# Where the activation tiles of a two-block fp32 transformer kernel start within 64 bytes of SBUF address

## The chip, the cores and the metric

The kernel runs on one core of a Trainium2 chip. The metric is the device time of one launch in microseconds (us); durations of single instructions are in nanoseconds (ns). Three runs of the kernel before gave 2814.7, 2814.81 and 2817.35 us; their median is 2814.81 us.

## The reference, cut to what matters

Two transformer blocks follow each other on 256 tokens of width 2048, all in float32. The first has a stick-breaking attention, a gated spatial branch and a squared-ReLU feed-forward part; the second has a modulation by projected vectors, a neighbourhood attention with a context of 256 more tokens, Fourier and Hyena mixers, and a gated feed-forward part with a short convolution:

```python
x = x + merged @ w_out
h2 = rms_norm(x, g_ff)
x = x + jnp.square(jax.nn.relu(h2 @ w_ff1)) @ w_ff2        # 2048 -> 8192 -> 2048
...
x = x + g1 * (y @ w_out)
x = x + g2 * conv_gated_mlp(modulate(rmsnorm(x, norm2_g), sh2, sc2), w_up, conv_w, conv_b, w_down)
return rmsnorm(x, final_norm_g)                            # inner width 5632
```

Nearly all the arithmetic is in the products of 256 rows of activations with large weight matrices.

## The kernel before

**Tiling.** Activations are held transposed, as tiles of 128 partitions by (chunk, 256 tokens); a chunk is one kilobyte in a partition. A weight matrix is streamed through in loads of 1 MB, [128, 4 chunks, 512 columns], each of which is one *product* (`product`, from line 1607 on). SyncE starts the load into one of four `RAW` buffers (`load`).

**Split numbers.** Each float32 operand is split into a high and a low part of type fp32r. For weights, ScalarE copies RAW to `WH` (`high_half`, line 477) and VectorE subtracts to get `WL` (line 882); both are double buffered. For activations the high parts are `XH`, `HH`, `MH`, `CH`, the low parts `XL`, `HL`, `ML`, `CL`. A product is high·high + high·low + low·high, three matmuls for each tile.

**Two forms of a product.** In `ws` (lines 1589 to 1591) a 128x128 piece of the weights is the stationary operand and 256 columns of activations move past it; a product has 4 chunks x 4 column pieces x 3 = 48 such matmuls, each with its own weight load. In `tok` (lines 1600 to 1602) a 128x128 piece of the activations is stationary and 512 columns of weights move; a product has 4 x 2 x 3 = 24 of them. In the profile's rows the moving operand's name stands first: `PS<-XH,WH` is `ws`, `PS<-WH,XH` is `tok`.

**Which tile serves where.** XH and XL hold the input of most products: projections, gates, first feed-forward matrices, the second block's w_out. HH and HL hold the hidden activations of the two feed-forward parts (`down`). MH and ML serve the first block's w_out alone, CH and CL the context's projections; in these last, one product with CH/CL and one with XH/XL take turns on the same weight tiles.

**Addresses.** Every tile lies at a place written out by hand, `at(name, shape, offset)`, 16512 bytes (258 x 64) above the start of a partition. The offsets of RAW, WH, WL, XH, XL, HH and HL are whole kilobytes. MH, ML, CH and CL lie whole kilobytes above `AR`, and `AR` is 128·1024 + 2176 + 5664, which leaves 32 when divided by 64. Rows of all these tiles and the slices of WH and WL that a matmul reads begin at multiples of 512 bytes from the tile's start.

**Order of work.** Each engine runs its own written-out program; semaphores join them. TensorE waits for `lo_done` (the weights' low half) before each half product, ScalarE waits for `pe_half` before it overwrites a WH half, VectorE waits for ScalarE. The two feed-forward parts are hardware loops over pairs of steps. Between stages a norm has to be finished (`norm_window`) before products go on.

Of the kernel before, what the change touches and what calls it, by code (L numbers as in the profile page):

```python
# [8 lines left out]
P = 128  # L9
T = 256  # L10
TT = T // P
D = 2048
KC = D // P
NB = 512
FT = NB // P
# [6 lines left out]
FNG = 4  # L22
HW = 512
# [127 lines left out]
def build_program(nc, d, out):  # L151
    f32, f32r = mybir.dt.float32, mybir.dt.float32r
# [5 lines left out]
    with ExitStack() as ctx:  # L158
        def at(name, shape, offset, dt=f32):
            return nc.alloc_sbuf_tensor_at(name, shape, dt, offset=base + offset)  # L160
# [4 lines left out]
        K = 1024  # L165
# [2 lines left out]
        WH = at("WH", [P, 2, FT, NB], 32 * K, f32r)  # L168
        WL = at("WL", [P, 2, FT, NB], 48 * K, f32r)
        X = at("X", [P, KC, T], 64 * K)  # L170
        XH = at("XH", [P, KC, T], 80 * K, f32r)
        XL = at("XL", [P, KC, T], 96 * K, f32r)
        HH = at("HH", [P, 2, FT, T], 112 * K, f32r)
        HL = at("HL", [P, 2, FT, T], 120 * K, f32r)
        NT = at("NT", [P, KC, T], 112 * K)
        CON = 128 * K
        cols = at("cols", [P, NCOLS], CON)
        small = CON + 2176
        mats = at("mats", [P, 4, P], small)
# [27 lines left out]
        lnb = at("lnb", [P, 1024], AR + 44 * K)  # L207
        bsp = at("bsp", [P, 8, P], AR + 48 * K)
        wsp = at("wsp", [P, 8, P], AR + 52 * K)
        t1 = 112 * K  # L210
        sgt = at("sgt", [P, 2, 2, T], t1 + 8 * K)
        qk_sq = at("qk_sq", [P, FT, T], t1)
        zs, zneg, lk, lsg, aw = (at(n, [P, 384], t1 + 1536 * k)
# [30 lines left out]
        P2 = at("P2", [P, 2, 2 * T], t1 + 4 * K)  # L244
        PT = at("PT", [P, 2, 4, T], t1 + 8 * K)
        SM = at("SM", [P, KC, T], AR + 8 * K)
        fcl = at("fcl", [P, TT, 2 * T], 80 * K)
        fcd = at("fcd", [P, 2, P], 84 * K)
        fU = at("fU", [P, FNG, 2 * T], 88 * K)
        KS = at("KS", [P, 2, 5, HW], AR + 24 * K)  # L250
        zt = at("zt", [P, TT, HW], AR + 44 * K)
        YS = at("YS", [P, 4, HW], AR + 48 * K)
        hSD = at("hSD", [P, 2, 2, TT, HW], 80 * K)
        dec = at("dec", [P, 2, TT, HW], 96 * K)
        Ef = at("Ef", [P, TT, 6 * P], 104 * K)
        pz = at("pz", [33, T], 110 * K)
        w1h = at("w1h", [33, 64], 111 * K)
        w2h = at("w2h", [64, 64], 111 * K + 512)
        w3h = at("w3h", [64, 2048], t1)
        hdn = at("hdn", [64, 2, T], AR + 52 * K)  # L260
        sr = at("sr", [64, 2, T], AR + 54 * K)
# [64 lines left out]
        def _(sp):  # L326
# [132 lines left out]
            for n in range(4):  # L459
                sp.wait_ge(sm["norm_h"], QUARTERS[N_LAST] + n + 1)  # L460
                sp.dma_start(out.rearrange("(k p) t -> p k t", p=P)[:, 4 * n:4 * n + 4, :],
                             NT[:, 4 * n:4 * n + 4, :]).then_inc(sm["outs"], 16)
            sp.wait_ge(sm["outs"], 64)

        @block.scalar
        def _(act):
# [25 lines left out]
            def root(n, total):  # L492

                act.wait_ge(sm["norm_sum"], n + 1)
                if n:
                    act.wait_ge(sm["norm_h"], QUARTERS[n])
                own.did(A(rt[:, 0:T], bank(SUM_BANK[n])[:, 0:T], ACT.Ln, bias=epsc[:, 0:1], scale=1.0 / total))
                own.settle()
                A(rt[:, 0:T], rt[:, 0:T], ACT.Exp, scale=-0.5).then_inc(sm["norm_rt"], 1)  # L499

            def split_high(dst, src, n):

                A(dst[:, 4 * n:4 * n + 4, :], src, ACT.Copy).then_inc(x_hi, 1)

            def shifted_high(dst, src, shift, norm, n):

                act.wait_ge(sm["norm_h"], QUARTERS[norm] + n + 1)
                for k in range(4 * n, 4 * n + 4):
                    ins = A(dst[:, k, :], src[:, k, :], ACT.Identity, bias=shift(k))
                ins.then_inc(x_hi, 1)  # L510

            def norm_window(norm, e, c, shift=None):

                def first_high():

                    for h in range(2):
# [4 lines left out]
                        if shift is None:  # L521
                            ins = A(XH[:, 2 * h:2 * h + 2, :], NT[:, 2 * h:2 * h + 2, :], ACT.Copy)
                        else:
                            for k in (2 * h, 2 * h + 1):
                                ins = A(XH[:, k, :], NT[:, k, :], ACT.Identity, bias=shift(k))
                        ins.then_inc(x_hi if h else first_hi, 1)

                def quarter_high(n):
                    if shift is None:
                        act.wait_ge(sm["norm_h"], QUARTERS[norm] + n + 1)  # L530
                        split_high(XH, NT[:, 4 * n:4 * n + 4, :], n)
                    else:
                        shifted_high(XH, NT, shift, norm, n)

# [54 lines left out]
            def branch_high(n):  # L589

                done(Place(C_OAB - 4 + n))
                if n == 0:
                    act.wait_ge(sm["o_done"], HEADS)
                    act.wait_ge(sm["s_done"], 4)
                split_high(XH, (qT if n < 2 else uT)[:, 4 * (n % 2):4 * (n % 2) + 4, :], n)

# [54 lines left out]
            def hidden_high(j):  # L651
                act.wait_ge(sm["relu_sq"], j.value(1, 1))
                if j.since(1):
                    act.wait_ge(sm["hid_lo"], j.value())
                A(HH[:, j.base % 2], FQ[:, :, :], ACT.Copy).then_inc(sm["hid_hi"], 1)

# [154 lines left out]
            for n in range(2):  # L811
                act.wait_ge(sm["norm_h"], QUARTERS[N_A] + n + 1)
                split_high(XH, SM[:, 4 * n:4 * n + 4, :], n)
            root(N_F, 512)
# [22 lines left out]
            def hidden_high2(q, j):  # L837
                act.wait_ge(acc_free[q.slot], q.turns(2, 1))
                A(HH[:, j.base % 2], FQ[:, :, :], ACT.Copy).then_inc(sm["hid_hi"], 1)

# [29 lines left out]
        def _(dve):  # L870
# [26 lines left out]
            def quarter(x, n):  # L897
                return x[:, 4 * n:4 * n + 4, :]
# [27 lines left out]
            def split_low(e, hi, lo, src, n):  # L926
                dve.wait_ge(x_hi, 4 * e + n + 1)
                tt(quarter(lo, n), src, quarter(hi, n).bitcast(f32), ALU.subtract).then_inc(x_lo, 1)

            def shifted_low(e, hi, lo, src, shift, n):  # L930
                dve.wait_ge(x_hi, 4 * e + n + 1)
                for k in range(4 * n, 4 * n + 4):
                    ins = stt(lo[:, k, :], src[:, k, :], shift(k), hi[:, k, :].bitcast(f32), ALU.add, ALU.subtract)
                ins.then_inc(x_lo, 1)

            def norm_window(norm, e, c, gain, finish, shift=None):

                def quarter_low(n):
                    if shift is None:
                        split_low(e, XH, XL, quarter(NT, n), n)  # L940
                    else:
                        shifted_low(e, XH, XL, NT, shift, n)

                def first_low(h):
# [6 lines left out]
                    if shift is None:  # L951
                        ins = tt(XL[:, t, :], NT[:, t, :], XH[:, t, :].bitcast(f32), ALU.subtract)
                    else:
                        for k in (2 * h, 2 * h + 1):
                            ins = stt(XL[:, k, :], NT[:, k, :], shift(k), XH[:, k, :].bitcast(f32),
                                      ALU.add, ALU.subtract)
# [143 lines left out]
            def branch_low(n):  # L1100
                split_low(E_OAB, XH, XL, quarter(qT if n < 2 else uT, n % 2), n)

# [81 lines left out]
            def hidden_low(j, before=0):  # L1184
                dve.wait_ge(sm["hid_hi"], j.value(1, before + 1))
                tt(HL[:, j.base % 2], FQ[:, :, :], HH[:, j.base % 2].bitcast(f32), ALU.subtract)\
                    .then_inc(sm["hid_lo"], 1)
# [223 lines left out]
            def products(o):  # L1411
                dve.wait_ge(sm["zf_ps"], o + 1)
                dve.wait_ge(sm["ks_done"], 5 * o + 5)
                dve.wait_ge(sm["hf_done"], 4)
                if o:
                    dve.wait_ge(sm["ys_done"], o)
                    dve.wait_ge(sm["hz_done"], o)
                re, im = PS[:, 4:6, :], PS[:, 6:8, :]
                own.did(tt(pp[:, 0], re, KS[:, o, 0:2, :], ALU.mult))
                own.did(tt(pp[:, 1], im, KS[:, o, 2:4, :], ALU.mult))  # L1420
                own.settle()
                settled(tt(YS[:, 0:2, :], pp[:, 0], pp[:, 1], ALU.subtract))
                own.did(tt(pp[:, 0], re, KS[:, o, 2:4, :], ALU.mult))
                own.did(tt(pp[:, 1, 0, :], bank(6), KS[:, o, 4, :], ALU.mult))
                own.did(tt(pp[:, 1, 1, :], bank(7), KS[:, o, 1, :], ALU.mult))
                own.settle()
                tt(YS[:, 2:4, :], pp[:, 0], pp[:, 1], ALU.add).then_inc(sm["ys_done"], 1)
# [25 lines left out]
            for n in range(2):  # L1453
                split_low(E_OUT2, XH, XL, quarter(SM, n), n)
            products(1)
# [116 lines left out]
        def _(pe):  # L1572
# [57 lines left out]
            def down(c, q, j, s, before=0):  # L1630

                if s == 0:
                    pe.wait_ge(sm["hid_lo"], j.value(1, before + 1))
                product(c, q, s, HH[:, j.base % 2], HL[:, j.base % 2])

# [468 lines left out]
```

## Time and profile before

| what | value |
|---|---|
| runs, us | 2814.7, 2814.81, 2817.35 |
| median, us | 2814.81 |
| profiled execution, span from first to last instruction, us | 2811.5 |
| TensorE busy, share of the span | 97% |
| VectorE, ScalarE busy | 68%, 42% |
| mean granted TensorE clock | 0.985 |
| HBM traffic | 555.7 MB, 198 GB/s read and written |

The profiled execution is recorded by its span alone, which leaves out what lies before the first and after the last instruction; the median of the runs is 3.3 us above it. Ends of matmuls are modelled in this profile (a matmul is shown as 0.28 us long although the next starts 0.12 us after it), so the cost of a matmul on TensorE is read from the distance between starts, not from its length.

### The profile page before, as it was taken

What the parts mean: (1) busy time and instruction counts of PE and PEld (TensorE: products, weight loads), DVE (VectorE), ACT (ScalarE), POOL (GpSimd) and SP (SyncE); (2) the same over time, 40 slices, a digit from 0 to 9 for tenths busy, and PEclk for the clock granted to TensorE, in tenths of its full rate; (3) what the DMA queues carried; (4) which work ended last, traced back from release to release, by engine and by line L of the source; (5) the groups of instructions that cost most, each with busy time, mean ns of one, the idle gap of its engine ahead of it and who ended that gap; (6) DMA issues with size and microseconds to landing.
All of it is one profiled execution on the core that took longest, in us unless ns stands there. A gap on an engine that the chain in (4) does not pass through costs nothing. (4 is left out here: it accounts for less than half of the span.)

```text
span 2811.5 us, 51119 instructions
## 1 busy us (share of the span) xinstructions
PE 2733.0 (97%) x21116; PEld 2643.1 (94%) x21116; DVE 1900.2 (68%) x2409; ACT 1175.5 (42%) x1228; POOL 0.2 (0%) x4
## 2 busy tenths in 40 slices
PE   7999999998999999999999999999899999999998
PEld 7989999998999999999999899859899999999998
DVE  6778877886887777777872237755656665656566
ACT  4666554433543434343432234333444443434343
POOL 0000000000000000000000000000000000000000
PEclk9999999999999999999999999999999999999999
DMA  7665666665787777777752354404455554545453
GB/s 277 221 234 203 226 216 239 220 243 194 266 269 271 266 270 265 270 265 270 267 173 90 102 157 145 141 18 162 139 182 186 187 181 159 186 153 186 159 182 104
DMA packets 282685, 558.37 MB, mean 199 GB/s; under 512 B 10407, under 2 KB 16840, under 8 KB 282056
## 3 DMA queue, kind: packets, MB, share of 16 engines
q1 hardware_dynamic: 282104, 553.60, 57.5%
q8 instruction: 144, 2.36, 0.3%
q10 hardware_dynamic: 400, 2.11, 0.3%
q14 instruction: 37, 0.30, 0.0%
HBM read 553.57 MB, written 2.10 MB: 198 GB/s over the span
## 5 line engine op out<-in xcount | busy, mean ns | idle before, releaser
L882 DVE TENSOR_TENSOR WL<-RAW,WH 128x1024 fp32r<-128x1024 f32 x840 | 1019.9, 1223 | 746.6 <-ACT WH L477 736.7
L477 ACT ACTIVATE WH<-RAW 128x1024 fp32r<-128x1024 f32 x840 | 887.7, 1059 | 1459.5 <-PE PS L1591 1341.4
L1589 PE MATMUL PS<-XH,WH 128*128 128x256 f32 x4288 | 1231.5, 287 | 39.6 <-issue 26.9
L1590 PE MATMUL PS<-XL,WH 128*128 128x256 f32 x4288 | 1221.8, 285 | 0.0
L1591 PE MATMUL PS<-XH,WL 128*128 128x256 f32 x4288 | 1221.4, 285 | 0.0
L1589 PEld LDWEIGHTS PS<-XH,WH 128*128 128x128 f32 x4288 | 830.7, 194 | 44.9 <-issue 31.9
L1590 PEld LDWEIGHTS PS<-XL,WH 128*128 128x128 f32 x4288 | 830.9, 194 | 1.2 <-issue 0.7
L1591 PEld LDWEIGHTS PS<-XH,WL 128*128 128x128 f32 x4288 | 830.4, 194 | 0.0
L1589 PE MATMUL PS<-HH,WH 128*128 128x256 f32 x1728 | 489.3, 283 | 0.0
L1590 PE MATMUL PS<-HL,WH 128*128 128x256 f32 x1728 | 489.0, 283 | 0.0
L1591 PE MATMUL PS<-HH,WL 128*128 128x256 f32 x1728 | 489.0, 283 | 0.0
L1589 PEld LDWEIGHTS PS<-HH,WH 128*128 128x128 f32 x1728 | 331.3, 192 | 0.0
L1590 PEld LDWEIGHTS PS<-HL,WH 128*128 128x128 f32 x1728 | 331.3, 192 | 0.0
L1591 PEld LDWEIGHTS PS<-HH,WL 128*128 128x128 f32 x1728 | 331.3, 192 | 0.0
L1097 DVE SCALAR_TENSOR_TENSOR ada1c<-ada1b,ctmp,ada1c 128x512 f32<-128x512 f32 x240 | 164.4, 746 | 0.3
L1231 DVE SCALAR_TENSOR_TENSOR adac<-adab,ctmp,adac 128x512 f32<-128x512 f32 x224 | 157.2, 745 | 0.7 <-DMA adab<-in_ada_w 0.4
L1600 PE MATMUL PS<-WH,XH 128*128 128x512 f32 x224 | 89.3, 399 | 0.0
L1602 PE MATMUL PS<-WH,XL 128*128 128x512 f32 x224 | 87.5, 390 | 0.0
L1601 PE MATMUL PS<-WL,XH 128*128 128x512 f32 x224 | 87.4, 390 | 0.0
L1192 DVE TENSOR_TENSOR X<-PS,X 128x1024 f32<-128x1024 f32 x64 | 77.9, 1217 | 0.0
L1521 DVE SCALAR_TENSOR_TENSOR X<-PS,mod,X 128x256 f32<-128x256 f32 x176 | 72.7, 476 | 2.3 <-PE PS L1591 2.3
L1589 PE MATMUL PS<-MH,WH 128*128 128x256 f32 x256 | 72.1, 282 | 0.7 <-DVE WL L882 0.7
(240 smaller groups left out, 1882.7 us busy)
## 6 DMA issues: line engine op xcount, KB each, us to landing
RAW<-in_w_ff SPq DMA_DIRECT2D x128, 1024.0 KB, 5.2
RAW<-in_w_in SPq DMA_DIRECT2D x112, 1024.0 KB, 5.0
RAW<-in_w_up SPq DMA_DIRECT2D x88, 1024.0 KB, 4.8
adab<-in_ada_w SPq DMA_DIRECT2D x128, 512.0 KB, 4.6
RAW<-in_w_down SPq DMA_DIRECT2D x44, 1024.0 KB, 5.0
ada1b<-in_ada_w SPq DMA_DIRECT2D x64, 512.0 KB, 5.9
RAW<-in_w_out SPq DMA_DIRECT2D x32, 1024.0 KB, 5.1
RAW<-in_w_oa SPq DMA_DIRECT2D x8, 1024.0 KB, 5.2
```

The source lines that it names most:

```text
L477: A(WH[:, c.base % 2, hs], RAW[:, c.base % SLOTS, hs], ACT.Copy).then_inc(hi_done, 1)
L882: tt(WL[:, b, hs], RAW[:, c.base % SLOTS, hs], WH[:, b, hs].bitcast(f32), ALU.subtract)\
L1097: stt(acc, w, x, acc, ALU.mult, ALU.add)
L1192: tt(quarter(X, s), acc_ws(q.slot), quarter(X, s), ALU.add).then_inc(acc_free[q.slot], 1)
L1231: ins = ts(acc, w, x, None, ALU.mult) if n == 0 else stt(acc, w, x, acc, ALU.mult, ALU.add)
L1521: ins = stt(X[:, 4 * s + k, :], acc_ws(q.slot)[:, k, :], mod[:, 5 * KC + 4 * s + k, 0:1], X[:, 4 * s + k, :], ALU.mult, ALU.add)
L1589: MM(out[:, f, :], wh, xh, start=first and f % 2 == 0, stop=False, skip_group_check=True)
L1590: MM(out[:, f, :], wh, xl, start=False, stop=False, skip_group_check=True)
L1591: ins = MM(out[:, f, :], wl, xh, start=False, stop=last, skip_group_check=True)
L1600: MM(out[:, t, :], h, wh, start=first, stop=False)
L1601: MM(out[:, t, :], h, wl, start=False, stop=False)
L1602: ins = MM(out[:, t, :], l, wh, start=False, stop=last)
```

## The change

Tiles move by some bytes, and nothing else. The instructions of every engine and their order stay as they were.

| tiles | start before, modulo 64 | start after, modulo 64 |
|---|---|---|
| RAW, WH, WL, X | 0 | 0 |
| XH, XL | 0 | 32 |
| HH | 0 | 16 |
| HL | 0 | 48 |
| MH, ML, CH, CL and all else above AR | 32 | 32 (128 bytes higher) |
| NT and the other temporaries in HH's place | 0 | 0 (64 bytes higher) |
| cols, mats and other constants | 0 | 0 (128 bytes higher) |
| tables in XH's and XL's place (fcl, fcd, fU, hSD, dec, Ef, pz, w1h, w2h) | 0 | 32 |

HH and HL are declared with four unused elements (16 bytes) ahead of the data: HH is 64 + 16 bytes above its old place, HL 96 + 16.

```diff
-        XH = at("XH", [P, KC, T], 80 * K, f32r)
-        XL = at("XL", [P, KC, T], 96 * K, f32r)
-        HH = at("HH", [P, 2, FT, T], 112 * K, f32r)
-        HL = at("HL", [P, 2, FT, T], 120 * K, f32r)
-        NT = at("NT", [P, KC, T], 112 * K)
-        CON = 128 * K
+        XH = at("XH", [P, KC, T], 80 * K + 32, f32r)
+        XL = at("XL", [P, KC, T], 96 * K + 32, f32r)
+        def hidden_half(name, offset, skip):
+            t = at(name, [P, skip + 2 * FT * T], offset, f32r)
+            return t[:, skip:].rearrange("p (b f t) -> p b f t", b=2, f=FT)
+
+        HH = hidden_half("HH", 112 * K + 64, 4)
+        HL = hidden_half("HL", 120 * K + 96, 4)
+        NT = at("NT", [P, KC, T], 112 * K + 64)
+        CON = 128 * K + 128
...
-        t1 = 112 * K
+        t1 = 112 * K + 64
...
-        hSD = at("hSD", [P, 2, 2, TT, HW], 80 * K)
-        dec = at("dec", [P, 2, TT, HW], 96 * K)
-        Ef = at("Ef", [P, TT, 6 * P], 104 * K)
+        hSD = at("hSD", [P, 2, 2, TT, HW], 80 * K + 32)
+        dec = at("dec", [P, 2, TT, HW], 96 * K + 32)
+        Ef = at("Ef", [P, TT, 6 * P], 104 * K + 32)
...
```

The tables left out (fcl, fcd, fU, pz, w1h, w2h) get the same + 32.

## Rows read from the trace of the kernel before

**Rows 1.** The page: busy time of each engine, and its line of granted clock
```profile
PE 2733.0 (97%) x21116; PEld 2643.1 (94%) x21116; DVE 1900.2 (68%) x2409; ACT 1175.5 (42%) x1228; POOL 0.2 (0%) x4
...
PEclk9999999999999999999999999999999999999999
```

**Rows 2.** The page: the chain that ended last, shares of the span
```profile
PE PS L1589 10%; PE PS L1590 10%; PE PS L1591 10%; PE PS L1932 1%; PE PS L1662 1%; PE PS L1950 0%; PE PS L1943 0%; PE PS L1868 0%; DVE NT L922 0%; PE PS L1825 0%; PE PS L1918 0%; ACT L499 0%; DVE WL L882 0%; ACT WH L477 0%; DVE hfb L1404 0%
```

**Rows 3.** Waits: waiter <- awaited: us in total, times, longest us
```profile
ACT WH L477 <- PE PS L1591: 1341.4, 729, 10.5
DVE WL L882 <- ACT WH L477: 736.7, 485, 8.7
...
PE PS L1589 <- DVE WL L882: 4.2, 4, 2.3
```

**Rows 4.** Groups of TensorE by line and shape: xcount | busy us, mean ns | idle before
```profile
L1589 PE MATMUL PS<-XH,WH 128*128 128x256 f32 x4288 | 1231.5, 287 | 39.6 <-issue 26.9 <-DVE XL L952 7.0 <-DVE WL L882 3.5
...
L1589 PE MATMUL PS<-HH,WH 128*128 128x256 f32 x1728 | 489.3, 283 | 0.0
...
L1600 PE MATMUL PS<-WH,XH 128*128 128x512 f32 x224 | 89.3, 399 | 0.0
...
L1589 PE MATMUL PS<-MH,WH 128*128 128x256 f32 x256 | 72.1, 282 | 0.7 <-DVE WL L882 0.7
...
L1589 PE MATMUL PS<-CH,WH 128*128 128x256 f32 x128 | 36.1, 282 | 0.0
...
L1600 PE MATMUL PS<-WH,CH 128*128 128x512 f32 x64 | 25.2, 394 | 0.0
```

**Rows 5.** Timeline of TensorE, first feed-forward part, XH/XL moving: start us, us, instruction
```profile
999.80 0.28 PE L1589 MATMUL PS<-XH,WH 128*128 128x256 f32 x1
...
1002.92 0.28 PE L1591 MATMUL PS<-XH,WL 128*128 128x256 f32 x1
```

**Rows 6.** Timeline of TensorE, the same part, HH/HL moving
```profile
980.00 0.28 PE L1589 MATMUL PS<-HH,WH 128*128 128x256 f32 x1
...
981.92 0.28 PE L1590 MATMUL PS<-HL,WH 128*128 128x256 f32 x1
```

**Rows 7.** Timeline of TensorE, the first block's w_out, MH/ML moving
```profile
630.00 0.28 PE L1589 MATMUL PS<-MH,WH 128*128 128x256 f32 x1
...
632.47 0.28 PE L1589 MATMUL PS<-MH,WH 128*128 128x256 f32 x1
```

**Rows 8.** Timeline of TensorE, context projections, form ws: starts of four successive products
```profile
1475.61 0.28 PE L1589 MATMUL PS<-CH,WH 128*128 128x256 f32 x1
...
1481.24 0.28 PE L1589 MATMUL PS<-XH,WH 128*128 128x256 f32 x1
...
1487.00 0.28 PE L1589 MATMUL PS<-CH,WH 128*128 128x256 f32 x1
...
1492.63 0.28 PE L1589 MATMUL PS<-XH,WH 128*128 128x256 f32 x1
```

**Rows 9.** Timeline of TensorE, context projections, form tok: starts of three successive products
```profile
1571.40 0.40 PE L1600 MATMUL PS<-WH,XH 128*128 128x512 f32 x1
...
1576.89 0.39 PE L1600 MATMUL PS<-WH,CH 128*128 128x512 f32 x1
...
1582.49 0.40 PE L1600 MATMUL PS<-WH,XH 128*128 128x512 f32 x1
```

**Rows 10.** Groups of VectorE and ScalarE by line and shape
```profile
L928 DVE TENSOR_TENSOR XL<-NT,XH 128x1024 fp32r<-128x1024 f32 x6 | 7.3, 1219 | 0.0
...
L928 DVE TENSOR_TENSOR ML<-ga,MH 128x1024 fp32r<-128x1024 f32 x4 | 4.9, 1220 | 0.0
...
L503 ACT ACTIVATE MH<-ga 128x1024 fp32r<-128x1024 f32 x4 | 4.2, 1054 | 2.5 <-DVE ga L1137 2.5
```

**Rows 11.** Stretches: us, busy of PE, PEld, DVE, ACT, POOL (x), PEclk, DMA share, GB/s
```profile
1000.00:1100.00 100.00, 100.00 (x837) 100.00 (x836) 77.19 (x84) 40.07 (x39) 0.00 (x0) 1.00 0.79 268
...
2479.00:2489.00 10.00, 6.92 (x30) 6.64 (x31) 1.39 (x4) 1.03 (x1) 0.00 (x0) 0.51 0.32 108
```

More of the change, by code:

```diff
@@ L246, in build_program @@
         SM = at("SM", [P, KC, T], AR + 8 * K)
-        fcl = at("fcl", [P, TT, 2 * T], 80 * K)
-        fcd = at("fcd", [P, 2, P], 84 * K)
-        fU = at("fU", [P, FNG, 2 * T], 88 * K)
+        fcl = at("fcl", [P, TT, 2 * T], 80 * K + 32)
+        fcd = at("fcd", [P, 2, P], 84 * K + 32)
+        fU = at("fU", [P, FNG, 2 * T], 88 * K + 32)
         KS = at("KS", [P, 2, 5, HW], AR + 24 * K)
@@ L252, in build_program @@
         YS = at("YS", [P, 4, HW], AR + 48 * K)
-        hSD = at("hSD", [P, 2, 2, TT, HW], 80 * K)
-        dec = at("dec", [P, 2, TT, HW], 96 * K)
-        Ef = at("Ef", [P, TT, 6 * P], 104 * K)
-        pz = at("pz", [33, T], 110 * K)
-        w1h = at("w1h", [33, 64], 111 * K)
-        w2h = at("w2h", [64, 64], 111 * K + 512)
+        hSD = at("hSD", [P, 2, 2, TT, HW], 80 * K + 32)
+        dec = at("dec", [P, 2, TT, HW], 96 * K + 32)
+        Ef = at("Ef", [P, TT, 6 * P], 104 * K + 32)
+        pz = at("pz", [33, T], 110 * K + 32)
+        w1h = at("w1h", [33, 64], 111 * K + 32)
+        w2h = at("w2h", [64, 64], 111 * K + 32 + 512)
         w3h = at("w3h", [64, 2048], t1)
```

## The prediction
> **What bounds the kernel now.** I began with the page. TensorE is busy for 97% of the span at a clock that is full nearly throughout [rows 1], and the chain that ended last runs through the three matmul lines of the `ws` products, with every other entry at 1% or less [rows 2]. That share understates it, because the chain counts other pieces in smaller entries, so I went on to the waits. ScalarE stands 1341 us waiting for TensorE to release a weight buffer, VectorE 737 us for ScalarE, while TensorE waits 4.2 us in all for finished weights [rows 3]. The weight pipeline is ahead of TensorE; what sets the time is the rate at which TensorE starts one matmul after another. The groups say how many there are [rows 4]: each `ws` row shown is one of three alike (lines 1589, 1590, 1591), so XH/XL move in 3 x 4288 = 12864 matmuls, HH/HL in 3 x 1728 = 5184, MH/ML in 768, CH/CL in 384; and XH/XL are stationary in 3 x 224 = 672 matmuls of the `tok` form, CH/CL in 192.
>
> Then the timeline, for the distance between starts. With XH/XL moving, 26 distances take 1002.92 − 999.80 = 3.12 us, 120.0 ns each [rows 5]. With HH/HL, 16 distances take 1.92 us, 120.0 ns again [rows 6]. With MH/ML, 21 distances take 2.47 us, 117.6 ns [rows 7]. Shape, type, stationary tile and instruction are the same; what differs is where the moving tile lies. MH/ML start 32 bytes past a multiple of 64 and XH, XL, HH, HL at a multiple.
>
> The kernel holds a better comparison, in which the stage is the same too. In the context projections, products with CH/CL and with XH/XL take turns on one pair of weight tiles. The one that begins at 1475.61 with CH lasts 5.63 us, the one with XH at 1481.24 lasts 5.76, the one with CH at 1487.00 again 5.63 [rows 8]. Over 48 matmuls that is 117.3 ns against 120.0. CH/CL also start 32 bytes past a multiple of 64. I take 117.5 ns for such tiles, between the two readings, so a gain of 2.5 ns.
>
> The same alternation in the `tok` form goes the other way. There the activation is the stationary operand: the product with XH takes 1576.89 − 1571.40 = 5.49 us, that with CH 1582.49 − 1576.89 = 5.60 us [rows 9]. Over 24 matmuls that is 228.8 against 233.3 ns, a loss of 4.6 ns for a stationary tile 32 bytes off.
>
> **The change part by part.** No instruction is added, removed or reordered, so the whole sum is counts times differences of distance.
>
> 1. XH/XL as moving operand go from 0 to 32, the place that MH and CH have now. 12864 x 2.5 = 32.2 us saved.
> 2. XH/XL as stationary operand (`tok`): 672 x 4.6 = 3.1 us lost.
> 3. HH goes to 16 and HL to 48. No row shows a tile at either. If 16 and 48 cost what 0 does, nothing is saved; if they do what 32 does, 5184 x 2.5 = 13.0 us. On the dear side the nearest row is the `tok` one, 4.6 ns for 512 columns, so 2.3 for 256: 5184 x 2.3 = 11.9 us lost. On the cheap side, 256 more columns cost 228.8 − 120.0 = 108.8 ns [rows 5, 9], so 11.2 ns of each 120 are not columns; were they all to go, 5184 x 11.2 = 58 us. I take 13.0: in the rows the one place with all tiles at a multiple of 64 runs at exactly 120.0, and the one place off it that moves past such weights is cheaper, so leaving 0 is what the rows credit. Both ends stay for the range.
> 4. MH, ML, CH, CL, and everything else above AR, keep their remainder of 32 and move by 128 bytes: 0, with no row for or against beyond that both differ by 40 kilobytes from each other and give 117.6 and 117.3.
> 5. Tables and temporaries: their matmuls are few and their remainder matters to TensorE in a few dozen instructions; 0.
> 6. ScalarE and VectorE now write and read at other remainders. VectorE needs 1219 ns for XL at 0 and 1220 for ML at 32; ScalarE 1054 ns for MH [rows 10], within 1% of its other copies of this size. 0; and both have room: in the first feed-forward part, the fullest stage, VectorE is busy 77 of 100 us and the DMA engines 0.79 of the time [rows 11]. With TensorE 2% faster they come to 79 us and 0.81, so neither becomes the bound. Where a stall is late next it is the weights' low half (WL), on which TensorE waits 4.2 us now [rows 3].
> 7. Given back: in stages where TensorE meets an attention or norm chain of the other engines, a faster product makes the wait behind it longer. The groups' idle time is small, 39.6 us before the commonest matmul, most of it "issue", which does not depend on products [rows 4]. After such gaps the clock is at its lower level (1.2 GHz) for a while: the stretch from 2479 to 2489, in which TensorE also stands idle for 3 of 10 us, has 0.51 granted and 30 matmuls started [rows 11]. There a matmul is twice as long and I credit no gain. I allow 2 us for all of this.
>
> Sum: 32.2 + 13.0 − 3.1 − 2 = 40.1 us. The span of the profiled execution is 2811.5 us, 3.3 under the median of the runs; from the median, 2814.8 − 40 = **2775 us**.
>
> **A rule that speaks against it.** The Trainium skill, page "SBUF — State Buffer", section "SBUF: two separate sides", gives TensorE a port of its own and a second, independent read port for weight loads, and says that on the engines' side only the port pair of VectorE and GpSimd causes contention; its section "Specifications (TRN2)" counts in lines of 16 bytes, and 16, 32 and 48 are whole such lines. By that the change would do nothing, and the time would be 2815. The 5.63 against 5.76 us on the same weights [rows 8] is what speaks against reading it so. The page "TensorE: Matmul & The Clock Gate" of the Trainium skill, section "Wait — 56ns, not 53.3ns?", gives columns divided by 2.4 GHz plus about 2.5 ns as the distance between starts, 109.2 ns for 256 columns, an estimate from that page; at 109.2 the 18048 matmuls would save 195 us. The 120.0 and 117.3 ns here show that it is not reached with a weight load at every matmul, at either place seen.
>
> **The rivals.**
> - *X gains, H does not* (the two places that no row shows are as dear as 0, or dearer). 2775 + 13 = 2788, and up to 2800 with H dearer by 2.3 ns. For it: no tile lies there. Chance 0.27.
> - *H gains twice what X does or more*, because its high and low tile now also differ from each other: 2775 − 13 = 2762, or less. For it: 11.2 ns that are not columns remain. Against it: the tiles at 32 only won 2.5 of them. Chance 0.08.
> - *Nothing happens*: what makes MH and CH faster is not the 32 but their place in larger units. From WH they lie 160 bytes off in units of 256, while XH will lie 32 off; if it is the 128 in this that counts, XH stays at 120 ns: about 2815 to 2818 with the loss of the `tok` form. This is also how the change fails to do what it says. Against it: only that 32 is the smallest step by which they differ. Chance 0.06.
> - *Slower*: an operand off a multiple of 64 costs time on every matmul, as the `tok` rows show for a stationary one, and the gain of MH and CH comes from the 128. At 2.3 ns each, 18048 moving matmuls lose 41.5 us, with `tok` 3.1 more: 2859. It decides as soon as XH's distance is above 120.3 ns (then the loss passes 5.6 us). For it: 5.60 against 5.49 us [rows 9]. Against it: CH moving is faster, not slower. Chance 0.04.
>
> **How the numbers follow.** The forecast (X and H both gain 1.5 to 3.5 ns) has 0.55. The range must reach the two neighbouring cases: low, H at twice the gain and X at 2.9 ns instead of 2.5, 2775 − 13 − 5 = 2757; high, H dearer by 2.3 ns, 2800. Left out are the last two rivals and the tail of the third. A measurement of this kernel can tell 0.2%, 5.6 us, from no change. Faster by more: 0.55 + 0.27 + 0.08 = 0.90; within: 0.06; slower: 0.04.
>
> **What would show it.** In the profile after, 27 successive starts with XH/XL moving span 3.05 us instead of 3.12, and vary by a few ns instead of being even; products with CH and with XH in the context stage last the same, 5.63 us; a `tok` product with XH takes 5.60. A `down` product with HH/HL takes 5.76 now; 5.64 is the forecast, 5.76 the first rival, 5.51 or less the second. The stretch of 100 us in the first feed-forward part holds 850 to 858 matmuls instead of 837. I am wrong if XH's distance stays at 120.0 ns, or if new waits of TensorE on WL take over 10 us.

## The result, and the profile after

The changed kernel takes 2772.61 us in the median of four runs (2771.69 to 2777.27), the one before 2816.08 in the median of its four (2814.7 to 2817.86). The ratio is 0.9851, 95% interval [0.9837, 0.9865]. That is 42 us less by the ratio (the medians are 43.5 apart), where 40 were forecast. One execution in the experiments below, the sixth of `k1_x_only_again`, took 3321.93 us at a granted clock of 0.746, where the others had 0.983 and more, and is in no ratio. Lines of the changed kernel's profile are four further on: 1593 to 1595 are the `ws` products, 1604 to 1606 the `tok` products.

The page: what bounds the kernel has not changed.

```profile
span 2770.0 us, 51119 instructions
...
PE 2688.8 (97%) x21116; PEld 2596.0 (94%) x21116; DVE 1899.6 (69%) x2409; ACT 1176.2 (42%) x1228; POOL 0.2 (0%) x4
...
PE PS L1593 10%; PE PS L1595 10%; PE PS L1594 10%; PE PS L1936 1%; PE PS L1954 1%; PE PS L1947 1%; PE PS L1666 0%; PE PS L1872 0%; DVE NT L926 0%; PE PS L1922 0%; ACT L503 0%; DVE WL L886 0%; PE PS L1829 0%; ACT WH L481 0%; DVE hfb L1408 0%
```

The counts and the other engines' work are those of [rows 1]; the span is 41.5 us shorter. It has gone from TensorE's own pace, as the timeline of TensorE shows (start us, us, instruction). First the four `down` products of one step of the first feed-forward part, HH/HL moving:

```profile
1000.47 0.28 PE L1593 MATMUL PS<-HH,WH 128*128 128x256 f32 x1
...
1023.09 0.28 PE L1593 MATMUL PS<-XH,WH 128*128 128x256 f32 x1
```

192 matmuls in 22.62 us, 117.8 ns each, against 120.0 in [rows 6]. Then the context projections, the place of [rows 8, 9], in the `ws` form (CH and XH taking turns) and in the `tok` form:

```profile
1451.00 0.28 PE L1593 MATMUL PS<-XH,WH 128*128 128x256 f32 x1
...
1456.60 0.28 PE L1593 MATMUL PS<-CH,WH 128*128 128x256 f32 x1
...
1462.20 0.28 PE L1593 MATMUL PS<-XH,WH 128*128 128x256 f32 x1
...
1540.60 0.40 PE L1604 MATMUL PS<-WH,XH 128*128 128x512 f32 x1
...
1546.20 0.40 PE L1604 MATMUL PS<-WH,CH 128*128 128x512 f32 x1
```

The product with XH lasts 5.60 us and so does that with CH: the difference of 0.13 us that [rows 8] had between them is gone. The `tok` product with XH lasts 5.60 us instead of 5.49.

XH's `ws` product does not always last 5.60 us, though. In the feed-forward part, one that follows HH/HL takes 5.65:

```profile
1023.09 0.28 PE L1593 MATMUL PS<-XH,WH 128*128 128x256 f32 x1
...
1028.74 0.28 PE L1593 MATMUL PS<-XH,WH 128*128 128x256 f32 x1
```

That is 116.7 ns a matmul in the one place and 117.7 in the other. Over the trace X runs at 116.7 ns in 109 products and at 117.8 in 156, and hardly ever between; its mean of 117.3 is a mixture of two levels. All products with M and C are at 116.7.

The gain exists at the full clock alone. In the stretches at the lower clock (granted 0.5) six distances take 1.28 us, 213.3 ns each, in the kernel before (its lines come first) as in the changed one:

```profile
2481.20 0.41 PE L1589 MATMUL PS<-XH,WH 128*128 128x256 f32 x1
...
2482.48 0.41 PE L1589 MATMUL PS<-XH,WH 128*128 128x256 f32 x1
```

```profile
2450.45 0.41 PE L1593 MATMUL PS<-XH,WH 128*128 128x256 f32 x1
...
2451.73 0.41 PE L1593 MATMUL PS<-XH,WH 128*128 128x256 f32 x1
```

The stretch that [rows 11] show holds 852 matmuls instead of 837, VectorE is at 78.79 of 100 us and the DMA engines at 0.79:

```profile
1000.00:1100.00 100.00, 100.00 (x852) 100.00 (x851) 78.79 (x88) 42.17 (x41) 0.00 (x0) 1.00 0.79 273
```

Of TensorE's waits the one on the weights' low half is the one that was expected to grow. It has gone from 4.2 us [rows 3] to 5.4:

```profile
PE PS L1593 <- DVE WL L886: 5.4, 4, 2.8
```

**The terms, over the whole trace.** Here and below a *pace* is the mean distance between starts over all matmuls of one kind at the full clock, gaps longer than a quarter of the usual distance left out.

| term | forecast, us | pace before, ns | pace after, ns | measured, us |
|---|---|---|---|---|
| XH/XL moving, 12864 | −32.2 | 119.96 | 117.34 | −33.7 |
| HH/HL moving, 5184 | −13.0 | 120.00 | 117.82 | −11.3 |
| XH/XL stationary, 672 | +3.1 | 228.0 | 233.3 | +3.5 |
| MH, ML, CH, CL moving, 1152 | 0 | 117.5 | 116.7 | −0.9 |

They add up to −42.4 us, where the span fell by 41.5. What is left over, 0.9 us, is the net of parts that were not told apart: TensorE's idle time before the commonest matmul grew from 39.6 us [rows 4] to 41.7, and the stretches at the lower clock shrank from 85 us to 78.

### The profile page after: what moved, and what is told of

Same layout as the page of the kernel before. It is cut to its first block and busy times, and to the rows that moved or that the text cites. A ratio compares the mean times of both kernels' runs of the same rounds, so it can differ in the third digit from the quotient of the medians.

```text
span 2770.0 us, 51119 instructions
## 1 busy us (share of the span) xinstructions
PE 2688.8 (97%) x21116; PEld 2596.0 (94%) x21116; DVE 1899.6 (69%) x2409; ACT 1176.2 (42%) x1228; POOL 0.2 (0%) x4
## 5 line engine op out<-in xcount | busy, mean ns | idle before, releaser
L1593 PE MATMUL PS<-XH,WH 128*128 128x256 f32 x4288 | 1217.2, 284 | 41.7 <-issue 27.6
L1595 PE MATMUL PS<-XH,WL 128*128 128x256 f32 x4288 | 1207.6, 282 | 0.0
L1594 PE MATMUL PS<-XL,WH 128*128 128x256 f32 x4288 | 1203.4, 281 | 0.0
L1593 PEld LDWEIGHTS PS<-XH,WH 128*128 128x128 f32 x4288 | 814.4, 190 | 47.5 <-issue 33.4
L1594 PEld LDWEIGHTS PS<-XL,WH 128*128 128x128 f32 x4288 | 814.9, 190 | 1.2 <-issue 0.7
L1595 PEld LDWEIGHTS PS<-XH,WL 128*128 128x128 f32 x4288 | 813.9, 190 | 0.0
L1594 PE MATMUL PS<-HL,WH 128*128 128x256 f32 x1728 | 480.6, 278 | 0.0
L1594 PEld LDWEIGHTS PS<-HL,WH 128*128 128x128 f32 x1728 | 325.4, 188 | 0.0
L1593 PEld LDWEIGHTS PS<-HH,WH 128*128 128x128 f32 x1728 | 324.5, 188 | 0.7 <-DVE X L1196 0.6
L1595 PEld LDWEIGHTS PS<-HH,WL 128*128 128x128 f32 x1728 | 324.6, 188 | 0.0
```

The source lines that it names most:

```text
L1593: MM(out[:, f, :], wh, xh, start=first and f % 2 == 0, stop=False, skip_group_check=True)
L1594: MM(out[:, f, :], wh, xl, start=False, stop=False, skip_group_check=True)
L1595: ins = MM(out[:, f, :], wl, xh, start=False, stop=last, skip_group_check=True)
```

## The experiments

All kernels compute the same values with the same instructions; only offsets differ. From here on a tile's place is given as its **distance** from the start of WH, and by units of 256 bytes, for reasons that the runs will show: before, X and H (XH/XL and HH/HL) are at 0, M and C at 160; after, X is at 32, HH at 80, HL at 112, M and C at 32 (160 + 128 − 256). In every experiment the tiles above AR lie 128 bytes higher, as in the changed kernel, unless said otherwise. Edits are shown against the changed kernel, that of `e0_ar_only` against the kernel before; most lines of the temporaries and tables that move along with these tiles are left out.

### One half of the change at a time

`e1_x_only`: H goes back to a multiple of 64. Because XL needs 32 bytes more room, this multiple is 64 bytes up.

```diff
-        HH = hidden_half("HH", 112 * K + 64, 4)
-        HL = hidden_half("HL", 120 * K + 96, 4)
+        HH = hidden_half("HH", 112 * K + 64, 0)
+        HL = hidden_half("HL", 120 * K + 64, 0)
```

> XH and XL at 32, HH and HL at 0 again. Theory 'each tile by its own place' : ws with XH/XL keeps the 117.3 ns of the changed kernel, ws with HH/HL goes back to 120.0, tok with XH stays at 233.3. The changed kernel's X terms are 12864 x 2.6 = 33.7 us gained and 672 x 5.3 = 3.5 us lost, so about 30 us under the kernel before: 2786 us, ratio 0.989. Rival 'the pair matters' (X products gain only because H, too, is off 0, or the whole comes from the 128-byte shift of the tiles above AR): XH/XL not at 117.3, or HH/HL not at 120.

Measured: 2755.95 us, ratio 0.9801 [0.9772, 0.9831]. That is faster than the whole change. X kept its pace (117.0 ns), `tok` its 233.3, but H did not go back to 120: its four products of one step take 21.77 us, 113.4 ns a matmul.

```profile
995.20 0.28 PE L1593 MATMUL PS<-HH,WH 128*128 128x256 f32 x1
...
1016.97 0.28 PE L1593 MATMUL PS<-XH,WH 128*128 128x256 f32 x1
```

Over the trace H runs at 115.1 ns, and this mean hides two levels: of 108 products, 65 are at 113.3 and 42 at 117.8, with one at 117.9. So the expectation failed on H, and with it the idea that places which are multiples of 64 are all alike. X has levels too, at its distance of 32: 116.7 ns in 208 products, 117.8 in 48, and 120.0 in the eight that follow the first H products of the second feed-forward part, here one of them with 5.76 us for 48 matmuls:

```profile
2080.07 0.28 PE L1593 MATMUL PS<-XH,WH 128*128 128x256 f32 x1
...
2085.83 0.28 PE L1593 MATMUL PS<-XH,WH 128*128 128x256 f32 x1
```

`e2_h_only`: X back at 0, H at the same remainders by 64 as in the change, but 64 bytes lower.

```diff
-        XH = at("XH", [P, KC, T], 80 * K + 32, f32r)
-        XL = at("XL", [P, KC, T], 96 * K + 32, f32r)
-        HH = hidden_half("HH", 112 * K + 64, 4)
-        HL = hidden_half("HL", 120 * K + 96, 4)
+        XH = at("XH", [P, KC, T], 80 * K, f32r)
+        XL = at("XL", [P, KC, T], 96 * K, f32r)
+        HH = hidden_half("HH", 112 * K, 4)
+        HL = hidden_half("HL", 120 * K + 32, 4)
```

> HH at 16 and HL at 48, XH and XL at 0 again. By its own place: HH/HL 117.8 ns, XH/XL 120.0, tok 228. 5184 x 2.2 = 11.3 us under the kernel before: 2804 us, ratio 0.996. Rival: HH/HL back at 120, no difference. e1 and e2 together should give the 42 us of the whole change within 3 us.

Measured: 2801.46 us, ratio 0.9951 [0.9935, 0.9968]. H at 117.8 ns, X at 119.9, `tok` 227.6. H's part of the change stands alone and has the size of the table's term. The gains of e1 and e2, 60 and 14 us by the medians, do not add up to the 42 that were expected, because H in e1 is at 64 and not at 0. X's part is read from e2 against the whole change: 0.9951 to 0.9851, 28 us, where the table's two terms for X give 30. No run has X at 32 with H at 0.

`e0_ar_only`: the kernel before with the tiles above AR 128 bytes higher and nothing else.

```diff
-        CON = 128 * K
+        CON = 128 * K + 128
```

> Only the constants and all tiles above AR lie 128 bytes higher; MH, ML, CH, CL keep 32 modulo 64. If only the remainder by 64 counts, MH/ML and CH/CL stay at 117.5 ns and the time at that of before (ratio 1.000). If something larger than 64 counts as well, they fall to the 116.7 ns of the changed kernel, which is 1 us in all, less than the time can show; the distances between starts must tell it.

Measured: 2813.98 us, ratio 0.9992 [0.9982, 1.0001]. X and H at 120.0; M at 116.95 instead of 117.50 (116.7 in 12 products, 117.8 in 4), C at 117.45, hardly moved. The 128-byte shift brings nothing that the time can show.

### Whose place is it?

`e4_w_at_32`: the weights' tiles move instead of the activations'. X and H are 64 bytes up, to make room, so their distance from the weights is 64 − 32 = 32; M and C are now at 288 − 32 = 256, which is 0 by units of 256.

```diff
-        WH = at("WH", [P, 2, FT, NB], 32 * K, f32r)
-        WL = at("WL", [P, 2, FT, NB], 48 * K, f32r)
-        X = at("X", [P, KC, T], 64 * K)
-        XH = at("XH", [P, KC, T], 80 * K + 32, f32r)
-        XL = at("XL", [P, KC, T], 96 * K + 32, f32r)
+        WH = at("WH", [P, 2, FT, NB], 32 * K + 32, f32r)
+        WL = at("WL", [P, 2, FT, NB], 48 * K + 32, f32r)
+        X = at("X", [P, KC, T], 64 * K + 64)
+        XH = at("XH", [P, KC, T], 80 * K + 64, f32r)
+        XL = at("XL", [P, KC, T], 96 * K + 64, f32r)
...
+        HH = hidden_half("HH", 112 * K + 64, 0)
+        HL = hidden_half("HL", 120 * K + 64, 0)
```

> WH and WL at 32, XH, XL, HH, HL at 0 (64 bytes higher), MH, ML, CH, CL at 32. Theory 'only the difference between the moving and the stationary start counts': ws with X and H falls to about 117.4 ns, ws with M and C, now both at 32, rises to 120.0, tok with X (stationary 0, moving 32) goes to 233 and tok with C to 227 or 228; time 18048 x 2.6 - 3.5 = 43 us under before, 2772 us. Theory 'a moving tile gains off 0 and a stationary one loses off 0': ws with X and H is at 120 ns or above, up to 122.6 if the tok loss of 5.3 ns per matmul is halved with the columns (time up to 2863 us), tok with X falls below 227, tok with C lies between.

Measured: 2773.94 us, ratio 0.9848 [0.9824, 0.9872]. The timeline shows the two families with their parts exchanged. In the `ws` form the product with XH lasts 5.66 us and the one with CH 5.75; in the `tok` form the one with CH lasts 5.45 and the one with XH 5.59:

```profile
1447.40 0.28 PE L1593 MATMUL PS<-XH,WH 128*128 128x256 f32 x1
...
1453.06 0.28 PE L1593 MATMUL PS<-CH,WH 128*128 128x256 f32 x1
...
1458.81 0.28 PE L1593 MATMUL PS<-XH,WH 128*128 128x256 f32 x1
...
1543.30 0.39 PE L1604 MATMUL PS<-WH,CH 128*128 128x512 f32 x1
...
1548.75 0.39 PE L1604 MATMUL PS<-WH,XH 128*128 128x512 f32 x1
...
1554.34 0.39 PE L1604 MATMUL PS<-WH,CH 128*128 128x512 f32 x1
```

Paces: X 117.0, H 117.0, M 119.9, C 119.9, `tok` X 233.2, `tok` C 227.3. X and H lie at multiples of 64 and are fast; M and C lie 32 off and are slow. M and C have the same addresses as in the changed kernel, where they took 116.7 ns. What counts is the distance between the moving and the stationary tile, in both forms: of the distances seen so far, 0 is the slowest for `ws` and the fastest for `tok`. The theory that a moving tile gains by itself and a stationary one loses wanted 120 ns or more for X and H and under 227 for `tok` X, and is refuted by these three; M, C and `tok` C came out where it, too, could have put them.

### How far, and by what unit

Three kernels put X and H together at other distances: `f1_x64_h64` at 64, `f3_x96_h96` at 96, `f2_x128_h128` at 128. The edit of the first; the others have 96 or 128 in the place of 64, and the temporaries with them:

```diff
-        XH = at("XH", [P, KC, T], 80 * K + 32, f32r)
-        XL = at("XL", [P, KC, T], 96 * K + 32, f32r)
-        HH = hidden_half("HH", 112 * K + 64, 4)
-        HL = hidden_half("HL", 120 * K + 96, 4)
+        XH = at("XH", [P, KC, T], 80 * K + 64, f32r)
+        XL = at("XL", [P, KC, T], 96 * K + 64, f32r)
+        HH = hidden_half("HH", 112 * K + 64, 0)
+        HL = hidden_half("HL", 120 * K + 64, 0)
```

> XH, XL, HH, HL all 64 bytes beyond a multiple of 128 from the weights. e1 had HH/HL there and they took 113.4 ns in some stretches and 117.8 in others, 115.1 in the mean. Theory 'the distance from the weights counts by units of 128, and 64 is the cheapest': X takes 113.4 to 117.8 as well, H too; with 115.1 for both the time is 2756 - 12864 x 1.9 = 2732 us, between 2709 and 2766 us at the two ends. Theory 'by units of 64, and H was fast in e1 for another reason' (remainder 0 as before): X goes back to 120 ns and the time to about 2790 us.

> XH, XL, HH, HL at 96. By units of 128, 96 is as far from the weights' place as 32 on the other side: if the sign does not count, X and H take 117 to 117.5 ns, tok X 233, time 18048 x 2.7 - 3.5 = 45 us under before, 2770 us. If only the way forward from the weights counts, 96 differs from 32 by more than 1 ns in either direction.

> XH, XL, HH, HL 128 bytes beyond where they were before. By units of 128: 120.0 ns for X and H as before, tok X 227 to 228, time 2814 us. By units of 256 or more: X and H below 118 ns, time under 2780 us.

At 64: 2778.81 us, ratio 0.9869 [0.9853, 0.9886]; H at 117.8 in all 108 products, X at 117.8 in 246 products and at 113.3 in 13. At 96, in one run, 2821.84 us: X and H at 120.0 ns, and `tok` X at 234.2, so all the gain is gone and the loss stays. Its four H products of one step take 23.04 us:

```profile
968.19 0.29 PE L1593 MATMUL PS<-HH,WH 128*128 128x256 f32 x1
...
991.23 0.29 PE L1593 MATMUL PS<-XH,WH 128*128 128x256 f32 x1
```

At 128, in one run, 2796.55 us: X at 118.8, H at 118.7. The same place in its timeline shows 22.78 us:

```profile
1005.23 0.28 PE L1593 MATMUL PS<-HH,WH 128*128 128x256 f32 x1
...
1028.01 0.28 PE L1593 MATMUL PS<-XH,WH 128*128 128x256 f32 x1
```

So 128 is not 0: the unit is not 128. In e4 C at 256 ran as slowly as X at 0, and its `tok` form at 227.3 ns, which otherwise only distance 0 gave, so 256 fits as the unit; and 96 is not the mirror of 32. By a unit of 128, f2 should have shown 120.0 ns and f3, with 96 as the mirror of 32, 117 to 117.5; neither came, and neither did "under 118 ns" for a larger unit; the other branch of f3, that 96 differs from 32 by over 1 ns, held. f1 came out by neither of its theories: H and nearly all of X at 117.8, and a time between 2766 us, the slow end of the one, and 2790 of the other.

`f4_all_64` is f1 with AR 32 bytes higher, which puts M and C at 64 too.

```diff
-        CON = 128 * K + 128
+        CON = 128 * K + 160
```

> As f1, and MH, ML, CH, CL, too, moved to 64 from the weights by units of 128 (AR 32 bytes higher). M and C go from 116.7 to between 113.4 and 117.8 ns, tok C shows the price of 64 for a stationary activation: 233 if any place off the weights' costs the same, less or more if it follows the distance. Time like f1 within 4 us: 1152 matmuls of M and C times at most 3.3 ns.

Measured: 2780.13 us, ratio 0.9877 [0.9861, 0.9894]. M and C run at 117.8 in all 24 products, X at 113.3 in six of the first stage, where no product with another tile has come before; `tok` C, stationary at 64, takes 233.3, the same as at 32 and at 160.

### Several paces at one distance

The distance alone does not fix the pace. At 32 the runs so far have 116.7, 117.8 and 120.0 ns; at 64 there are two paces, 113.3 and 117.8. The runs of this part go after the second pair. In f1 the fast one was seen, among other places, in the context projections, where products with CH (distance 32) come before those with XH: 5.45 us for 48 matmuls.

```profile
1453.00 0.28 PE L1593 MATMUL PS<-XH,WH 128*128 128x256 f32 x1
...
1458.45 0.28 PE L1593 MATMUL PS<-CH,WH 128*128 128x256 f32 x1
```

In e1 it was seen where H (at 64) follows X (at 32). That suggested that a tile at 64 keeps the pace it is entered with. `h1_x64_h32` exchanges the places of e1; the hidden tiles' 16 KB now lie ahead of X's.

```diff
-        XH = at("XH", [P, KC, T], 80 * K + 32, f32r)
-        XL = at("XL", [P, KC, T], 96 * K + 32, f32r)
+        XH = at("XH", [P, KC, T], 96 * K + 64, f32r)
+        XL = at("XL", [P, KC, T], 112 * K + 64, f32r)
...
-        HH = hidden_half("HH", 112 * K + 64, 4)
-        HL = hidden_half("HL", 120 * K + 96, 4)
-        NT = at("NT", [P, KC, T], 112 * K + 64)
+        HH = hidden_half("HH", 80 * K + 32, 0)
+        HL = hidden_half("HL", 88 * K + 32, 0)
+        NT = at("NT", [P, KC, T], 80 * K)
```

> The places of e1 exchanged: XH/XL at 64 from the weights, HH/HL at 32 (the hidden tiles' 16 KB now lie ahead of XH's and XL's). Theory 'tiles at 64 keep the pace they are entered with': entered from products whose tiles are at 32 they take 113.4 ns, entered from a gap or from one another 117.8 (as H after X in e1, X after C in f1). Then the X products that directly follow H products in the feed-forward parts take 113.4, all others 117.8, and H takes 116.7 to 117.8: in the first part that is 3 or 4 of 4 products in each step, as far as the one-column matmuls between them do not break it; time under that of f1 (2779) by up to 12864 x 0.6 x 4.4 = 34 us, 2745 to 2775. Rival 'it is the tile, not the entry' (the hidden tiles are fast at 64 for a reason of their own): X stays at 117.8 everywhere, time 2779 less 5184 x 0.8 = 4, 2775 us.

Measured: 2767.42 us (2755.66 to 2772.92), ratio 0.9814 [0.9785, 0.9842]. In the profile X is at 113.3 in 44 products and at 117.8 in 214; H, now at 32, is at 116.7 in 95 products and at 120.0 in 12, a level that the expectation did not have. So it is not the tile: X can have the fast pace. But coming after H is not enough, either. In the second feed-forward part three steps have X fast behind H and the later ones not; in the first part X is at 117.8 behind H in nearly every step, as at 1021.43. The entry theory is half right at best: the offset of the product before doesn't decide it.

`h2_xh32_xl64` and `h3_xh64_xl32` place the high and the low tile of X differently (H at 64).

```diff
-        XL = at("XL", [P, KC, T], 96 * K + 32, f32r)
+        XL = at("XL", [P, KC, T], 96 * K + 64, f32r)
```

```diff
-        XH = at("XH", [P, KC, T], 80 * K + 32, f32r)
-        XL = at("XL", [P, KC, T], 96 * K + 32, f32r)
+        XH = at("XH", [P, KC, T], 96 * K + 64, f32r)
+        XL = at("XL", [P, KC, T], 80 * K + 32, f32r)
```

> As e1, but XL at 64 while XH stays at 32. If the pace follows from every matmul's own distance from the weights, X goes from 117.0 to a third of 113.4..117.8 and two thirds of 117.0, 115.8 to 117.3, and the time by at most -15 or +4 us from e1's 2756. If a jump of the moving tile by 32 bytes between matmuls matters by itself (as HH at 16, HL at 48 took 117.8 where both at 32 took 117.0), X is at 117.8 or above and the time 10 us above e1. H behind it shows what an entry from such products does: 113.4 or 117.8.

> The mirror of h2: XH at 64, XL at 32 (XL's 16 KB now ahead of XH's). By each matmul's own distance: two thirds at 64 and one at 32, between 114.6 and 117.5 ns, 2725 to 2763 us. If the middle matmul at 32 re-enters the two at 64 each time, they stay at 113.4 and the time is near 2725 us. If the jump costs by itself: 117.8 or above, 2766 us or more.

Measured: 2777.37 us, ratio 0.9869 [0.9853, 0.9886], and 2778.76 us, ratio 0.9866 [0.9849, 0.9882]. X at 117.8 in both, and H behind it at 117.8 in all 108 products. A tile pair that alternates between 32 and 64 has one pace only, the one that HH at 80 with HL at 112 has in the changed kernel, and HH at 16 with HL at 48 in e2; H at 64 never reached 113.3 after it. This is the outcome that was written down for "the jump costs by itself", but it does not show that cost: 117.8 is also a level of 32 alone and of 64 alone.

### The faster version again

`k1_x_only_again` is the kernel of e1, unchanged.

> The kernel of e1 a second time, with more rounds, since its runs went from 2754.8 to 2769.0 us and it is the fastest so far. If the fast pace of HH/HL (113.4 ns) is reached in most executions, the median stays near 2756 us, ratio 0.980, and single runs lie between 2753 and 2770. If it was luck of that series, the median goes to 2766, which is 2756 + 5184 x (117.0 - 115.1). In its profile HH/HL are at 113.4 in some products and 117.8 in the others, possibly not the same ones as in e1.

Measured: ratio 0.9814 [0.9793, 0.9834]; its runs in the ratio are 2752.08, 2756.46, 2762.15, 2763.01 and 2774.26 us, and their median lies between the 2756 and the 2766 of the two expectations. The profiled execution has a span of 2750.3 us with H at 113.3 to 113.4 in 83 products and at 117.8 in 25, so the share of fast products differs from that of e1 with the same program. X at 32 is at 116.7 in 201 products, at 117.8 in 39 and at 120.0 in 24. The groups of TensorE (xcount | busy us, mean ns | idle before) show where it is faster than the changed kernel. First the changed kernel, then this one:

```profile
L1593 PE MATMUL PS<-XH,WH 128*128 128x256 f32 x4288 | 1217.2, 284 | 41.7 <-issue 27.6
...
L1595 PE MATMUL PS<-HH,WL 128*128 128x256 f32 x1728 | 486.0, 281 | 0.0
```

```profile
L1593 PE MATMUL PS<-XH,WH 128*128 128x256 f32 x4288 | 1218.7, 284 | 40.8 <-issue 27.6 <-DVE XL L956 6.0 <-DVE WL L886 4.6
...
L1595 PE MATMUL PS<-HH,WL 128*128 128x256 f32 x1728 | 478.8, 277 | 0.0
```

X is about the same (as a pace 117.2 ns against 117.3), H is shorter by 4 ns (as a pace 114.4 against 117.8). Both series of this kernel lie below the changed kernel's interval [0.9837, 0.9865] with theirs ([0.9772, 0.9831] and [0.9793, 0.9834]): H at distance 64 behind X at 32 beats both kernels, by 10 to 14 us over the changed one, with a spread of 22 us between runs.

## Why the prediction was right, point by point

The time (2775 forecast, 2772.6 measured), the range and the sign held. By its steps:

- **What bounds the kernel**: right. TensorE's own pace had to set the time for a gain of 2.6 ns per matmul to arrive in full, and it did; the waits stayed.
- **Step 1, X moving**: right in size (2.6 ns), and right that TensorE's cost per matmul hangs on where the moving tile lies; the alternating products on one pair of weight tiles [rows 8] were the evidence. The rule was wrong, and that the number fits is in part luck. It was "off a multiple of 64": in e4 X lies at a multiple of 64 and takes 117.0 ns, because the weights are 32 off, and in f1, at 64, it takes 117.8. It was also "the place that MH and CH have now": they were at 160, with 117.5, and X went to 32, where 117.3 is the mean of 116.7 and 117.8. The rival of larger units was wrong in that X would stay at 120, but such units do matter: 128 bytes alone take X from 120.0 to 118.8 in f2, and M from 117.5 to 116.95 in e0.
- **Step 2, X stationary**: right, 5.3 ns instead of 4.6. The reason given, a loss for a stationary tile 32 bytes off, was wrong: in e4 CH, off by 32, was stationary at 227.3 ns, because the weights were off by as much.
- **Step 3, H**: size nearly right (2.2 ns instead of 2.5), rule wrong. It was argued that leaving 0 is what the rows credit. At 96 X and H have left 0 and take 120.0 ns as before, so leaving 0 alone brings nothing, and that the forecast for 16 and 48 held was luck. The other rivals for H had the right bounds: 113.3 ns, seen in e1, lies 6.7 ns below 120, inside the 11.2 that were reckoned as "not columns".
- **Step 4, M, C**: taken as 0, measured 0.9 us gained. e0 showed the shift alone to be worth 0.5 ns for M and none for C, so it takes X's move as well to bring C to 116.7.
- **Steps 5 to 7**: held in their terms. VectorE and the DMA engines came out at 79 of 100 us and 0.79 of the time; the wait on WL is 5.4 us. Step 6 read its room from a stretch that is not the fullest of that part: from 773 to 843 of the kernel before, VectorE was busy 61.5 of 70 us, 88%, and the DMA engines 0.82. It did no harm, since the wait on WL hardly grew. The 2 us given back were not measured apart; the terms and the span leave 0.9 open. To credit no gain at the lower clock was right (213.3 ns before and after), but a matmul there is not twice as long: 213.3 against 120.0 is 1.8 times.
- **The rule that speaks against it**: by the Trainium skill's page "SBUF — State Buffer" (section "SBUF: two separate sides"), TensorE's reads of the moving tile and its weight loads go by independent ports. e4 shows that the pace depends on both addresses together: 117.9 ns for XH against 119.8 for CH in turns on the same weights, with the order reversed by moving the weights. Whether it is at these ports that the two meet, no run shows.

**What stays open.** Why 0 and 96 take 120.0, 128 mostly 118.7, 160 117.5, 64 either 113.3 or 117.8, and 32 either 116.7 or 117.8 and at times 120.0 was not explained, only mapped; distances of 192 and 224 were not tried, and 96 and 128 have one run each. What decides between the paces at 32 is open and was not followed up. What decides between those at 64 is open as well: not the tile (h1), not the program alone (e1 and its repetition differ in their shares), and not just the distance of the product before (h1).

## What to carry to other kernels

Where TensorE is the bound and each matmul has its own weight load, read the distance between starts, family by family, and look for tiles that differ only in address: two families taking turns on the same weights are an experiment that the kernel has already made. Then move the activations relative to the weights by 32 or 64 bytes, and measure the form in which the activations are stationary separately, since it pays where the other gains. A pattern read at one place says nothing of the next 32 bytes: each has to be run. And look at single products before trusting a mean: a mean pace can be a mixture of levels.

## What was not expected of the hardware

The distance between the starts of the moving and of the stationary tile sets at which paces fp32r matmuls of 256 columns with a weight load each can run, and these come in steps: 120.0 ns (0, 96, 256), mostly 118.7 (128), 117.8 or 116.7 and at times 120.0 (32), 117.5 (160), 117.8 (pairs such as 16 with 48, 80 with 112 or 32 with 64), 117.8 or in some stretches 113.3 (64). All of this holds at the full clock; at the lower one X takes 213.3 ns at 0 and at 32. With 512 columns and the activations stationary the order is another: 227 to 228 at 0, 232.6 at 128, 233.3 at 32, 64 and 160, 234.2 at 96. And one program can run at one of two paces in the same place: in e1's profile 65 of 108 products with H were fast, in its repetition 83.
